# Stage buffers by turns, mirrored key blocks, and another order of loads in a hybrid attention and convolution block

## Chip, core and metric

The kernel runs on one core of a Trainium2 chip. The metric is the device time of one execution in microseconds (us), the median of several executions. All times below are of the kernel before the change.

## What is computed

One residual block over 2048 frames of width 1024, in float32:

```
h = rmsnorm(x, pre_norm_w)
q, k, v, z_att, b, c, u, z_conv, g_att, g_conv = split(h @ w_in)
q, k = partial_rotary(q), partial_rotary(k)            # 8 heads of 64, rotary on 16 of them
pr = softmax(where(chunk(k) <= chunk(q), q k^T / 8, min))   # chunk = 64 frames
a = pr[even heads] - lam * pr[odd heads]               # 4 pairs of heads
att = rmsnorm(a @ v, subln_w) * 0.8 * silu(z_att)
cv = b * causal_conv3(c * u) * silu(z_conv)
m = sigmoid(g_att + bias0) * (att @ w_att_out) + sigmoid(g_conv + bias1) * (cv @ w_conv_out)
out = x + rmsnorm(m @ w_out, post_norm_w)
```

## The kernel before

Every large product is done in three float32r matmuls: each operand is split into a high and a low part (ScalarE copies the high part, VectorE subtracts to get the low one), and TensorE adds high times high, high times low and low times high into one bank of PSUM (`split_product`, lines 889 to 891). All DMAs are issued by one queue, SyncE's (SP), in an order written out by hand; each engine walks its own hand-written program and the programs meet at semaphores. There are four stages.

**First x tiles and V.** The 16 tiles of x (128 rows) are squared and summed (`norm_root`, ScalarE, line 1087, with a Sqrt at line 1090), scaled (`norm`, VectorE, line 1306), transposed (`turn_x`, TensorE, line 899) and split (`ht_split`). The weights of V come in four parts, `wv_raw` 0 to 3, each split into `wv_hi` (line 1106) and `wv_lo`. TensorE's program is `turn_x(0)`, `turn_x(1)`, `turn_x(2)`, V product of tile 0, `turn_x(3)`, V product of tile 1, and so on.

**Line tiles.** 28 tiles of 128 features (z, convolution, queries and keys) times 4 blocks of 512 frames, in the order `SEQ`: tile by tile, but for the last two tiles (p = 26 and 27) block by block, blocks 1, 2, 3, 0, each block with tile 26 and then 27. A block's result is split into one of four buffers, `stage[b]` with b the block, and stored to `qk_s` by 3 DMAs. ScalarE waits for the buffer's last store before it writes it again (`put_out`, line 1161, the ACTIVATE at line 1180). Between these stores SP issues what the next stage needs: keys and queries of the first pair of heads (lines 647 and 632), the weights of gate units 0 to 3 (`load_unit`, line 654; one unit is 24 matmuls, 1 MB of weights), V (line 638).

**Attention and gates.** TensorE does units 0 and 1, then rounds of scores (lines 947, 948), transposes (958), values (975) and a share of the 64 gate units (line 1010). There are 4 pairs of heads with 16 query tiles each. Pairs 1 and 3 go through the query tiles upwards, pairs 2 and 4 downwards. A query tile uses the key blocks (512 frames) up to its own frame, so a pair that goes downwards frees block 3 first and block 0 last, at its end. Key block c lies in `k_sl[c]`, value block c in `v_sl[c]`, and the next pair's block is loaded when the same block of this pair was used for the last time. VectorE masks and takes maxima (1514), ScalarE takes exponentials (1205) and copies finished gate units to `gate_st` (1243), from where SP stores them; before ScalarE copies a unit it waits for the store of the unit two before.

**Merge.** Four blocks of 512 frames. For each, 8 pairs of products (m = 0 to 7, two halves, lines 889 to 891 with `wa` and `br`) go to four banks in turn; the gates are read back through a ring of 5 buffers (`ring_load`, line 806), passed through Sigmoid (line 1269), multiplied (1598) and added (1601), and the sum is split into `m_hi` (1279) and `m_lo` (1603). A ring buffer is loaded again when its last reader is done. In the first block the rows of `w_out` are also loaded (`wo_raw`) and split (`wo_hi` 1282, `wo_lo` 1607), one after each m. Then follow the products with `w_out` (`rows`), Square with a sum (1289), Sqrt, reciprocal, a scaling by it and by `post_w` (1621), the addition of x (1629) and the store.

Of the kernel before, what the change touches and what calls it, by code (L numbers as in the profile page):

```python
# [77 lines left out]
RING = 5  # L78
USES = 2 * KT + 2 * QPB
# [33 lines left out]
def stores_before(p):  # L113
    return NT // 4 + sum(stores_of(x) for x in range(p))

# [15 lines left out]
class Plan:  # L131
# [96 lines left out]
def build(nc, t):  # L228

    with ExitStack() as whole:  # L230
# [86 lines left out]
        k_sl = [held(f"k_sl{i}", [P, 2, BLK], F32R, room) for i in range(NB)]  # L317
# [4 lines left out]
        v_sl = [held(f"v_sl{i}", [P, 2, QPB, VD], F32R, room) for i in range(NB)]  # L322
# [124 lines left out]
        unit_w = [sem(f"unit_w{i}") for i in range(2)]  # L447
        ht_in = [sem(f"ht_in{i}") for i in range(KT // 2)]
# [61 lines left out]
        def _(sp):  # L510
# [83 lines left out]
            def store_block(p, b):  # L594
                kind, j = kind_of(p), place_of(p)
                cs = slice(b * BLK, (b + 1) * BLK)
# [3 lines left out]
                if kind == "z":  # L600
                    sp.dma_start(z_s[p * P:(p + 1) * P, cs], stage[b][:, 0, :]).then_inc(stored[b], 16)
                elif kind == "conv":
                    c0 = (p - CONV_P) // 4 * P
                    sp.dma_start(cv_s[:, c0:c0 + P, cs].rearrange("s p e -> p s e"), stage[b][:]
                                 ).then_inc(stored[b], 16)
                elif j:
                    for lo, hi, row in segments(j):
                        sp.dma_start(qk_s[tile_of(p) // 4, :, row:row + hi - lo, cs].rearrange("s p e -> p s e"),
                                     stage[b][lo:hi]).then_inc(stored[b], 16)
                else:  # L610
                    for half in range(2):
                        rows = qk_s[tile_of(p) // 4, half, :, cs].rearrange("(h r) n -> h r n", r=HD)
                        for a in range(2):
                            sp.dma_start(rows[:, a * HALF:(a + 1) * HALF, :], stage[b][a * HD:(a + 1) * HD, half, :]
                                         ).then_inc(stored[b], 16)
# [14 lines left out]
            def load_k(pair, c):  # L630
                for half in range(2):
                    sp.dma_start(k_sl[c // BLK][half * HD:(half + 1) * HD].bitcast(F32),
                                 qk_s[1, half, pair * P:(pair + 1) * P, c:c + BLK].rearrange("(h j) n -> j h n", h=2)
                                 ).then_inc(k_loaded[c // BLK], 16)

            def load_v(pair, c):
                for half in range(2):
                    sp.dma_start(v_sl[c // BLK][:, half].bitcast(F32),  # L638
                                 v_s[half, c:c + BLK, pair * VD:(pair + 1) * VD].rearrange("(t p) e -> p t e", p=P)
                                 ).then_inc(v_loaded[c // BLK], 16)  # L640
# [10 lines left out]
            def load_unit(u):  # L651
                if u >= 4:
                    sp.wait_ge(unit_done, u - 1)
                sp.dma_start(unit_weights(u)[:].bitcast(F32),
                             split_s[u % GATE_TILES].rearrange("p s (k c) -> p s k c", k=KT)).then_inc(unit_w[u % 2], 16)
# [5 lines left out]
            for i, (p, b) in enumerate(SEQ[-2 * NB:]):  # L661
                store_block(p, b)
                if i == 1:
# [7 lines left out]
                    load_k(0, 0)  # L671
                    load_q(Plan(True), 1)
                if i == 3:
                    sp.wait_ge(proj_done, AT[LINE - 1, 2] + 1)
                    load_unit(0)
                    load_v(0, 0)
                    load_unit(1)
                    for c in range(BLK, S, BLK):
                        load_k(0, c)
                if i == 6:  # L680
                    sp.wait_ge(proj_done, AT[LINE - 2, 0] + 1)
                    load_unit(2)
                    for c in range(BLK, S, BLK):
                        load_v(0, c)
            sp.wait_ge(proj_done, AT[LINE - 1, 0] + 1)
            load_unit(3)
            for s_ in stored:
                sp.wait_ge(s_, 16 * stores_before(LINE))
# [23 lines left out]
            def load_wa(m):  # L712
                sp.dma_start(wa[m][:].bitcast(F32), split_s[GATE_TILES + m].rearrange("p s (k c) -> p s k c", k=KT)
                             ).then_inc(wa_in[wa_group(m)], 16)

# [20 lines left out]
            def attend(plan):  # L736
                gates((0, LEAD))
                for R in plan.rounds:
# [14 lines left out]
                    if R % 2 == 1 and 3 <= R <= TILES + 1:  # L753
# [9 lines left out]
                        for c in gone:  # L763
                            if 2 * B < TILES - NT:
                                load_v(2 * B // NT + 1, c * BLK)
                            elif c:
                                load_branch(0, (None, 7, 0, 1)[c])
# [7 lines left out]
                    for turn, score, value, part in plan.round(R):  # L775
                        gates(part)
                        if score and plan.last_use(G, score[0]):
                            c = score[0] // BLK
                            if pair < VH - 1:
                                sp.wait_ge(qk_done, 2 * (plan.before(G) + c + 1))  # L780
                                load_k(pair + 1, score[0])
                            elif c:
                                sp.wait_ge(qk_done, 2 * (plan.before(G) + c + 1))
                                load_branch(0, 3 + c)

            by_plan(sp, attend)

            def ring_load(n, i):
                b = NB - 1 - n
                place = ring_at(n, i)  # L790
                g = n * USES + i - RING
                if g >= 0:
                    was_n, was = divmod(g, USES)
                    if was >= 2 * KT:
                        sp.wait_ge(y_stored[place], 16 * rows_before(n, i))
# [886 lines left out]
```

## Time and profile before

| | us |
|---|---|
| median of 3 executions | 1841.86 (lowest 1839.49, highest 8872.33) |
| the profiled execution, its own time | 1842.11 |
| its span, first to last instruction | 1840.3 |
| TensorE busy | 1761.2 |
| VectorE busy | 891.5 |
| ScalarE busy | 581.8 |
| GpSimd busy | 89.0 |
| mean granted clock of TensorE | 0.986 of full |

The span is what the trace covers; 1.8 us lie around it. Busy times are sums over the span, so what bounds the kernel is read from the waits of the busiest engine, TensorE, and from what ended them.

### The profile page before, as it was taken

To read this page: it belongs to the slowest core of one execution; us is meant where nothing else is said; L and a number is where in the kernel's file an instruction comes from. 1 tells how busy PE (TensorE), PEld (TensorE's weight loads), DVE (VectorE), ACT (ScalarE), POOL (GpSimd) and SP (SyncE) were. 2 spreads that over 40 slices of the span, in tenths; PEclk is the share of its full clock that TensorE was granted. 3 is DMA by queue.
4 is the path that set the end of the run, shared out by engine and by line. 5 is a ranking of instruction groups with operands and counts; after the bars stand their busy time and mean duration, and the time that the engine had idled before them with its cause. 6 is when DMAs were issued, how large, how long until landed. Compare 5 with 4: busy or idle time off the path is not lost.

```text
span 1840.3 us, 22425 instructions
## 1 busy us (share of the span) xinstructions
PE 1761.2 (96%) x8512; PEld 1469.3 (80%) x8512; DVE 891.5 (48%) x1903; ACT 581.8 (32%) x1040; POOL 89.0 (5%) x74
## 2 busy tenths in 40 slices
PE   6999999999999999699999998999999979999998
PEld 5878888888888888588887887888788758888887
DVE  5538234444334411267666655766666434434252
ACT  5422112121101111144444443444354333313131
POOL 0000000000000000111101112111001000000000
PEclk9999999999999999899999999999999989999999
DMA  6438446465504546776575678657655775353532
GB/s 225 152 129 330 174 160 200 166 206 172 171 12 137 153 122 182 215 218 194 185 201 173 206 227 237 193 177 230 223 169 166 243 239 195 120 180 107 183 104 74
DMA packets 149574, 328.90 MB, mean 179 GB/s; under 512 B 14801, under 2 KB 68049, under 8 KB 135889
## 3 DMA queue, kind: packets, MB, share of 16 engines
q1 hardware_dynamic: 149458, 327.37, 56.3%
q8 instruction: 70, 1.15, 0.3%
q14 instruction: 46, 0.38, 0.1%
HBM read 216.16 MB, written 111.16 MB: 178 GB/s over the span
## 4 chain that ended last, share of the span: by engine, by line
PE 83%; DMA 6%; SPq 4%; ACT 3%; DVE 2%; issue 2%; DVEq 0%; ACTq 0%
PE bank L889 18%; PE bank L890 18%; PE bank L891 18%; PE bank L1010 15%; PE bank L975 5%; PE bank L947 3%; PE bank L948 3%; PE bank L958 2%; ACT e L1205 2%; DMA gate_s<-gate_st 1%; SPq L638 1%; DMA qk_s<-stage 1%; DMA ring<-gate_s 1%; PE bank L899 1%; DVE at_lo L1550 1%
## 5 line engine op out<-in xcount | busy, mean ns | idle before, releaser
L889 PE MATMUL bank<-ht,w 128*128 128x512 f32 x896 | 349.3, 390 | 2.6 <-issue 2.6
L890 PE MATMUL bank<-ht,w 128*128 128x512 f32 x896 | 349.3, 390 | 0.0
L891 PE MATMUL bank<-ht,w 128*128 128x512 f32 x896 | 349.1, 390 | 0.0
L1010 PE MATMUL bank<-ht,w 128*128 128x512 f32 x912 | 239.9, 398 | 1.2 <-DMA w<-split_s 1.2
L889 PEld LDWEIGHTS bank<-ht,w 128*128 128x128 f32 x896 | 168.5, 188 | 38.1 <-ACT w L1118 3.0
L891 PEld LDWEIGHTS bank<-ht,w 128*128 128x128 f32 x896 | 168.6, 188 | 35.1
L890 PEld LDWEIGHTS bank<-ht,w 128*128 128x128 f32 x896 | 168.5, 188 | 35.0
L1010 PEld LDWEIGHTS bank<-ht,w 128*128 128x128 f32 x912 | 168.5, 191 | 33.9 <-DMA w<-split_s 1.4
L1514 DVE CUSTOM_DVE_ANT_0 e<-bank,zeros 128x512 f32<-128x512 f32 x192 | 125.0, 688 | 130.4 <-PE bank L948 129.9
L1205 ACT ACTIVATE e<-e,nbias 128x128 f32<-128x128 f32 (+15 forms) x128 | 152.8, 1196 | 83.7 <-DVE nbias L1523 83.5
L1010 PE MATMUL bank<-hx,w 128*128 128x512 f32 x576 | 156.1, 399 | 3.9 <-DMA w<-split_s 3.9
L947 PE MATMUL bank<-k_sl,q_st 128*128 128x512 f32 (+3 forms) x320 | 129.3, 408 | 21.6 <-DVE stage L1427 8.3
L1214 ACT ACTIVATE at_hi<-bank 128x512 fp32r<-128x512 f32 (+3 forms) x160 | 83.2, 528 | 170.4 <-PE bank L958 170.3
L975 PE MATMUL bank<-at_hi,v_sl 128*128 128x256 f32 (+1 forms) x576 | 117.9, 283 | 12.0 <-DVE at_lo L1550 11.9
L1010 PEld LDWEIGHTS bank<-hx,w 128*128 128x128 f32 x576 | 105.5, 190 | 25.0 <-DMA w<-split_s 5.6
L878 POOL TENSOR_SCALAR mask<-kc,qc 128x128 f32<-128x128 f32 (+3 forms) x64 | 87.5, 1367 | 619.9 <-DVE mx L1514 619.3
L948 PE MATMUL bank<-k_sl,q_st 128*128 128x512 f32 (+3 forms) x320 | 117.1, 370 | 0.0
L889 PE MATMUL bank<-br,wa 128*128 128x512 f32 x256 | 101.0, 395 | 14.3 <-DVE ring L1598 13.6
L975 PEld LDWEIGHTS bank<-at_hi,v_sl 128*128 128x128 f32 x576 | 95.0, 190 | 23.7 <-DVE at_lo L1550 21.5
L1550 DVE TENSOR_TENSOR at_lo<-bank,at_hi 128x512 fp32r<-128x512 f32 (+3 forms) x160 | 97.1, 607 | 31.2 <-ACT at_hi L1214 30.8
L890 PE MATMUL bank<-br,wa 128*128 128x512 f32 x256 | 100.7, 394 | 0.0
L891 PE MATMUL bank<-br,wa 128*128 128x512 f32 x256 | 100.5, 393 | 0.0
(141 smaller groups left out, 2496.7 us busy)
## 6 DMA issues: line engine op xcount, KB each, us to landing
w<-split_s SPq DMA_DIRECT2D x62, 1024.0 KB, 5.4
split_s<-piece SPq DMA_DIRECT2D x24, 1024.0 KB, 5.0
q_st<-qk_s SPq DMA_DIRECT2D x128, 128.0 KB, 5.6
gate_s<-gate_st SPq DMA_DIRECT2D x64, 256.0 KB, 6.0
ring<-gate_s SPq DMA_DIRECT2D x64, 256.0 KB, 3.4
raw<-in_w_in SPq DMA_DIRECT2D x28, 512.0 KB, 6.2
ht_s<-ht SPq DMA_DIRECT2D x3, 4096.0 KB, 27.4
qk_s<-stage SPq DMA_DIRECT2D x48, 192.0 KB
```

Source lines behind the costliest of these rows:

```text
L878: nc.gpsimd.tensor_scalar(mask[m % 2][:, 0:wide], kc[:, c:c + wide], qc[:, plan.tile(G)[1]:plan.tile(G)[1] + 1], MASKED, ALU.is_gt, ALU.mu ...
L889: nc.tensor.matmul(out, left[0], right[0], start=start, stop=False)
L890: nc.tensor.matmul(out, left[0], right[1], start=False, stop=False)
L891: return nc.tensor.matmul(out, left[1], right[0], start=False, stop=stop)
L947: nc.tensor.matmul(out, q_st[G // 2 % 2][:, 0, h, qs], k, start=True, stop=False)
L948: nc.tensor.matmul(out, q_st[G // 2 % 2][:, 1, h, qs], k, start=False, stop=True).then_inc(qk_done, 1)
L975: return nc.tensor.matmul(bank[7][:, q0:QB], v, (at_lo if x == 1 else at_hi)[:, k, q0:QB], start=start, stop=stop)
L1010: mm = nc.tensor.matmul(bank[2 + u % 2][:], unit_weights(u)[:, term // 2, k, :], h_slot(bb, k)[:, term % 2, :], start=i == 0, stop=i == PE ...
L1205: nc.scalar.activation(e, e, ACT.Exp, bias=nbias[G % 2][:, h:h + 1], scale=SCALE, accum_out=esum[G % 2][:, h:h + 1]).then_inc(exp_done, 1)
L1214: nc.scalar.activation(at_hi[:, c // P:(c + wide) // P, q0:q0 + P], bank[5 + o % 2][:, 0:wide].rearrange("p (k n) -> p k n", n=P), ACT.Cop ...
L1514: nc.vector.tensor_tensor_reduce(e[:, c:c + wide], bank[(0, 1, 4)[o % 3]][:, 0:wide], mask[m % 2][:, 0:wide] if masked else zeros[:, 0:wid ...
L1550: nc.vector.tensor_tensor(at_lo[:, ks, q0:q0 + P], bank[5 + o % 2][:, 0:wide].rearrange("p (k n) -> p k n", n=P), at_hi[:, ks, q0:q0 + P]. ...
```

## The change

Four things are changed.

- The results of tiles 26 and 27 go to the stage buffers in the order 2, 3, 0, 1, 2, 3, 0, 1 (`stage_at`), not to the buffer of their block. Waits count the stores into that buffer (`stored_before`). Before attention VectorE waits for buffer 3 alone, not for all four.
- In pairs 3 and 4 of the heads key block c and value block c lie in slot 3 - c (`slot`). During pair 2 the slot that comes free is loaded with block 3 - c of pair 3 (`next_keys`). Buffers of the last stage lie over the slots, so the first merge block's inputs are loaded in the order that fits. The first two gate units get a semaphore of their own.
- At the start the four parts of V's weights are loaded before x tiles 1 to 3, ScalarE loads the table for Sqrt before anything else, and ScalarE and VectorE split V's weights between x tiles 0 and 1. TensorE's program there is unchanged.
- In the first merge block ring buffers 0 and 1 are loaded before the last gate unit is stored, 2 to 4 before any `wa`; `w_out` is loaded later and split later (`WO_AT`: none at m = 0 and 1, then 1, 1, 1, 1, 2 and 2). The row scaling is turned round: VectorE first multiplies by `post_w` in the bank (before the reciprocal is there) and then multiplies by the reciprocal and adds x in one instruction.

```diff
+WO_AT = ((), (), (0,), (1,), (2,), (3,), (4, 5), (6, 7))
...
+def stage_at(p, b):
+    return (2, 3, 0, 1)[(AT[p, b] - AT[LINE - 2, 1]) % 4] if p >= LINE - 2 else b
+
+def stored_before(p, b):
+    return NT // 4 + sum(stores_of(x) for x, y in SEQ[:AT[p, b]] if stage_at(x, y) == stage_at(p, b))
...
+    def slot(self, G, c):
+        return c // BLK if G < TILES // 2 else NB - 1 - c // BLK
+
+    def next_keys(self, G, c):
+        return S - BLK - c if G // NT == 1 else c
...
             for i in range(4):
                 sp.dma_start(wv_raw[i][:], t["w_v"][i]).then_inc(wv_loaded[i], 16)
-                if i < 3:
-                    load_x(i + 1)
+            for i in range(1, 4):
+                load_x(i)
...
                         for c in gone:
                             if 2 * B < TILES - NT:
-                                load_v(2 * B // NT + 1, c * BLK)
+                                load_v(plan, 2 * B // NT + 1, plan.next_keys(2 * B, c * BLK))
...
                             if pair < VH - 1:
                                 sp.wait_ge(qk_done, 2 * (plan.before(G) + c + 1))
-                                load_k(pair + 1, score[0])
+                                load_k(plan, pair + 1, plan.next_keys(G, score[0]))
...
+                sp.wait_ge(qk_done, 2 * plan.before(TILES))
+                for s_ in gate_stored:
+                    sp.wait_ge(s_, 16 * (UNITS - 6) // 2)
+                ring_load(0, 0)
+                ring_load(0, 1)
...
             store_gate(UNITS - 1)
+            sp.wait_ge(pv_done, PAIRS)
+            for i in range(2, RING):
+                ring_load(0, i)
             sp.wait_ge(unit_done, UNITS)
-            sp.wait_ge(pv_done, PAIRS)
+            load_wa(4)
+            for s_ in att_stored:
+                sp.wait_ge(s_, 16 * PAIRS // 2)
+            load_wo(0)
+            load_wo(1)
+            load_wa(5)
             for s_ in gate_stored:
                 sp.wait_ge(s_, 16 * UNITS // 2)
-            for i in range(RING):
-                ring_load(0, i)
-                if i < 4:
-                    load_wa(4 + i)
             for i in range(RING, 2 * KT):
                 ring_load(0, i)
                 if i == RING:
-                    for s_ in att_stored:
-                        sp.wait_ge(s_, 16 * PAIRS // 2)
-                if i < RING + KT:
-                    k = i - RING
-                    sp.dma_start(wo_raw[k][:], t["w_out"][k * P:(k + 1) * P, :]).then_inc(wo_in[k // 2], 16)
+                    load_wa(6)
+                    load_wo(2)
+                    load_wo(3)
+                elif i == RING + 1:
+                    load_wa(7)
+                elif i < RING + 6:
+                    load_wo(i - RING + 2)
...
+            nc.scalar.preload_act_table_set("sqrt_and_others")
             act.wait_ge(consts_ready, 4)
             norm_root(0)
-            norm_root(1)
...
+            split_wv(0)
+            split_wv(1)
             ht_split(0)
+            split_wv(2)
+            split_wv(3)
+            norm_root(1)
+            ht_split(1)
             norm_root(2)
-            ht_split(1)
             norm_root(3)
...
                 if kind != "conv":
-                    act.wait_ge(stored[b], 16 * stores_before(p))
+                    act.wait_ge(stored[st], 16 * stored_before(p, b))
...
-            for s_ in stored:
-                dve.wait_ge(s_, 16 * stores_before(LINE))
+            dve.wait_ge(stored[3], 16 * stored_in_all(3))
...
+                    dve.wait_ge(f_sq, n * 8 + 2 * i + 1)
+                    weigh(0)
                     dve.wait_ge(f_sq, n * 8 + 2 * (i + 1))
                     nc.vector.tensor_tensor(ss[:, 2:3], ss[:, 0:1], ss[:, 1:2], ALU.add).then_inc(f_sum, 1)
+                    weigh(1)
...
-                        nc.vector.tensor_tensor(ring[place][:], bank[4 + o % 4][:], ring[place][:], ALU.add
-                                                ).then_inc(f_out, 1)
+                        nc.vector.scalar_tensor_tensor(out=ring[place][:], in0=bank[4 + o % 4][:], scalar=ss[:, 2:3],
+                                                       in1=ring[place][:], op0=ALU.mult, op1=ALU.add
+                                                       ).then_inc(f_out, 1)
```

## Rows read from the trace of the kernel before

**Rows 1.** The page: busy time, share of the span, instructions of each engine
```profile
PE 1761.2 (96%) x8512; PEld 1469.3 (80%) x8512; DVE 891.5 (48%) x1903; ACT 581.8 (32%) x1040; POOL 89.0 (5%) x74
```
**Rows 2.** Waits of TensorE: total us, times, longest us
```profile
PE bank L899 <- DVE x_n L1306: 16.6, 2, 10.2
PE bank L889 <- DVE ring L1598: 13.6, 1, 13.6
...
PE bank L947 <- DVE stage L1427: 8.3, 1, 8.3
PE bank L947 <- DMA k_sl<-qk_s: 7.2, 1, 7.2
PE bank L947 <- DVE mx L1514: 6.1, 1, 6.1
```
**Rows 3.** Timeline, first 24 us: start us, us, engine, line, instruction [idle before, releaser]
```profile
6.85 1.28 ACT L1090 ACT_TABLE_LOAD   x1
...
9.08 1.06 ACT L1087 ACTIVATE x_n<-x_in 128x1024 f32<-128x1024 f32 x1 [0.64 <-DMA x_in<-in_x]
...
12.99 1.06 ACT L1106 ACTIVATE wv_hi<-wv_raw 128x1024 fp32r<-128x1024 f32 x1 [0.53 <-DMA wv_raw<-in_w_v]
...
17.46 1.06 ACT L1087 ACTIVATE x_n<-x_in 128x1024 f32<-128x1024 f32 x1
...
20.51 1.97 PE L899 MATMUL bank<-ident,x_n 128*128 128x128 f32 x8 [6.41 <-DVE x_n L1306]
...
22.13 0.78 PE L889 MATMUL bank<-wv_hi,ht 128*128 128x512 f32 x1
```
**Rows 4.** Timeline, line tiles to attention, TensorE, ScalarE, SP
```profile
739.70 10.13 PE L1010 MATMUL bank<-ht,first_w 128*128 128x512 f32 x44
...
748.44 1.09 ACT L1180 ACTIVATE stage<-bank 128x512 fp32r<-128x512 f32 x2 [23.38 <-DMA qk_s<-stage]
...
760.42 2.50 PE L1010 MATMUL bank<-ht,w 128*128 128x512 f32 x5 [1.23 <-DMA w<-split_s]
...
763.03 0.77 SPq L654 DMA_DIRECT2D w<-split_s  x1
...
777.14 0.60 ACT L1243 ACTIVATE gate_st<-bank 128x512 f32<-128x512 f32 x1 [2.27 <-PE bank L1010]
```
**Rows 5.** Chain of waits: ten gate matmuls at full clock
```profile
788.91 2.30 PE bank L1010 x10
```
**Rows 6.** Windows: us, busy of each engine, then clock, DMA share, GB/s
```profile
718.00:724.00 6.00, 6.00 (x28) 4.99 (x27) 0.00 (x0) 0.03 (x1) 0.00 (x0) 1.00 0.76 206
...
726.00:746.00 20.00, 20.00 (x90) 16.57 (x89) 0.00 (x0) 0.00 (x0) 2.53 (x4) 1.00 0.95 260
...
750.00:770.00 20.00, 4.58 (x13) 3.61 (x14) 2.19 (x10) 3.06 (x5) 0.29 (x1) 0.67 0.93 269
```
**Rows 7.** Landing times of the weights of units 2 and 3
```profile
DMA to landing us min/median/max: 7.1/7.8/8.4
```
**Rows 8.** Chain of waits between pairs 2 and 3
```profile
1113.17 4.13 PE bank L1010 x14
```
**Rows 9.** Chain of waits, first merge block
```profile
1474.98 10.61 DMA ring<-gate_s
...
1513.93 4.05 DMA ring<-gate_s
...
1520.01 3.95 DMA ring<-gate_s
```
**Rows 10.** Timeline, first merge block: TensorE, ScalarE, VectorE
```profile
1467.98 0.50 PE L889 MATMUL bank<-br,wa 128*128 128x512 f32 x1 [0.69 <-ACT gate_st L1243]
...
1495.10 1.06 ACT L1282 ACTIVATE wo_hi<-wo_raw 128x1024 fp32r<-128x1024 f32 x1 [8.25 <-DMA wo_raw<-in_w_out]
...
1536.29 1.23 DVE L1607 TENSOR_TENSOR wo_lo<-wo_raw,wo_hi 128x1024 fp32r<-128x1024 f32 x1 [0.26 <-ACT wo_hi L1282]
```
**Rows 11.** Timeline, end of the output, VectorE
```profile
1836.47 1.28 DVE L1629 TENSOR_TENSOR ring<-bank,ring 128x512 f32<-128x512 f32 x2
```

More of the change, by code:

```diff
@@ L316, in build @@
         q_st = [held(f"q_st{b}", [P, 2, 2, QB], F32R, room) for b in range(2)]
[L317 removed]
+        k_sl = {i: held(f"k_sl{i}", [P, 2, BLK], F32R, room) for i in (3, 0, 1, 2)}
         sub = ExitStack()
@@ L447, in build @@
         unit_w = [sem(f"unit_w{i}") for i in range(2)]
+        first_in = [sem(f"first_in{i}") for i in range(2)]
         ht_in = [sem(f"ht_in{i}") for i in range(KT // 2)]
@@ L714, in load_wa, with ring_load @@
                              ).then_inc(wa_in[wa_group(m)], 16)
+            def ring_load(n, i):
+                b = NB - 1 - n
+                place = ring_at(n, i)
+                g = n * USES + i - RING
+                if g >= 0:
+                    was_n, was = divmod(g, USES)
+                    if was >= 2 * KT:
+                        sp.wait_ge(y_stored[place], 16 * rows_before(n, i))
+                    elif was % 2:
+                        sp.wait_ge(m_sum, was_n * KT + was // 2 + 1)
+                    else:
+                        sp.wait_ge(m_lo_done, was_n * KT + was // 2 + 1)
+                if i < 2 * KT:
+                    r0 = (i % 2) * D + (i // 2) * P
+                    src = gate_s[r0:r0 + P, b * BLK:(b + 1) * BLK]
+                else:
+                    r0 = b * BLK + (i - 2 * KT) // 2 * P
+                    src = t["x"][r0:r0 + P, (i % 2) * 512:(i % 2) * 512 + 512]
+                sp.dma_start(ring[place][:], src).then_inc(ring_loaded[place], 16)
             def gates(part):
@@ L1319, in _, with split_wv @@
             dve.wait_ge(consts_ready, 4)
-            norm(0)
-            norm(1)
-            for r in range(4):
+            def split_wv(r):
                 dve.wait_ge(w_hi_done, r + 1)
@@ L1604, in _ @@
                                             ).then_inc(m_lo_done, 1)
-                    if n == 0:
-                        dve.wait_ge(wo_hi_done, m + 1)
-                        nc.vector.tensor_tensor(wo_lo[m][:], wo_raw[m][:], wo_hi[m][:].bitcast(F32), ALU.subtract
+                    for k in WO_AT[m] if n == 0 else ():
+                        dve.wait_ge(wo_hi_done, k + 1)
+                        nc.vector.tensor_tensor(wo_lo[k][:], wo_raw[k][:], wo_hi[k][:].bitcast(F32), ALU.subtract
                                                 ).then_inc(wo_lo_done, 1)
@@ L1619, in _ @@
                         o = 2 * i + half
-                        bk = bank[4 + o % 4][:]
-                        nc.vector.scalar_tensor_tensor(out=bk, in0=bk, scalar=ss[:, 2:3],
-                                                       in1=post_w[:, half * 512:half * 512 + 512], op0=ALU.mult,
-                                                       op1=ALU.mult).then_inc(f_scaled, 1)
-                    for half in range(2):
-                        o = 2 * i + half
                         place, count = ring_at(n, 2 * KT + o), ring_count(n, 2 * KT + o)
```

124 lines of the change are left out of this document (63 added, 61 removed).

## The prediction

> **What bounds the kernel now.** I read the page first: TensorE is busy 1761.2 of 1840.3 us [rows 1]. So the question is where it is not busy, and the view of its waits answers that [rows 2]: six waits make 51.8 us of the 79 that are left. Two stand at the very start (16.6), one is in the first merge block (13.6), two are between line tiles and attention (8.3 and 6.1), one is between pairs 2 and 3 of the heads (7.2). The timeline and the chain of waits around each show who was late. The change touches each of these places and nearly nothing else, so I go through them in order of time. I count against the profiled execution's own 1842.1 us, which is 0.2 above the median of the runs.
>
> A wait costs more than its length: after a long idle stretch TensorE's matmuls run at half clock. Ten gate matmuls take 2.30 us at full clock [rows 5], five after a stop take 2.50 [rows 4]. I therefore price a stall from the last matmul before it to a point behind it where the clock is full again, and compare with the same work at 0.23 us a matmul.
>
> **The start.** V's first product stands at 22.13, right behind the transposes of x tile 2 at 20.51 [rows 3], since TensorE's program has them first. They follow the Square of tile 2 (17.46) by 3.05 us. Today that Square waits behind the four weight splits. What lands when: x tile 1 is the fourth load and there at 9.08; the part of `wv_raw` that is seventh is there at 12.99. After the change x tile 1 is seventh, so I take 13.0 for it. Then: its Square at 13.0, its transposes 3.05 later at 16.05, its ScalarE split behind these (2.5 us until the second half is done, taken as for tile 2), Square of tile 2 at 18.55, its transposes at 21.6, V's product at 23.2. That is **+1.1 us**. Two table loads of 1.28 us [rows 3] leave the chain of tile 0, but tile 0 is early then and waits for tile 1: this part is worth nothing. Bounds: -1.5 (x tile 1 lands earlier than the rank says) and +1.5.
>
> On the landing order the Trainium skill, DMA: Bandwidth & Descriptors, section "Queues, rings and completion order", says that completion is not first in, first out for one issuing engine. By that rule tile 1 may overtake weights, and the term would be nearer to its lower bound; the nine landings in this trace came in issue order.
>
> **Line tiles to attention.** Stage buffer b serves tile 26 and then tile 27 of the same block, so ScalarE stood 23.38 us until a store landed [rows 4], and TensorE, whose units 0 and 1 ended at 739.70 + 10.13 = 749.83, waited 8.3 us for the last block. Then VectorE waited for all stores: 6.1 us more [rows 2], with 1.23 for unit 2's weights between [rows 4]. With four buffers by turns, each buffer's store is two blocks of 10.9 us old when it is needed. Both waits go. The whole stretch from 749.83 to the end of unit 2 at 777.14 [rows 4] holds 24 gate matmuls (5.5 us) and 13 small ones (1.8), 7.3 us at full clock: a possible gain of 27.3 - 7.3 = 20.0.
>
> What is late next is the DMA queue. Its engines are busy 0.95 in 726 to 746 and 0.93 in 750 to 770 [rows 6]; before and between, SP had nothing to issue because the stores waited. The first batch (units 0 and 1, V's first block, keys, two stores) is 19.0 us of work, the second (stores, units 2 and 3, the rest of V) starts at about 750.5. In the changed kernel the first follows straight on what fills 0.76 of 718 to 724 [rows 6], at about 722.8, and the second straight on the first at 741.8. Unit 3's weights were issued at 763.03 and took 8.4 us [rows 4, 7], so they landed 20.9 us after their batch began; less 0.8 us, since that batch was not full at its beginning, that gives 761.9. Unit 2's landed at 760.4 and now land, by the same shift, at 751.6 (wait 1.3 behind the first scores). TensorE wants unit 3 at 749.83 + 1.3 + 7.3 = 758.4 and gets it at 761.9: it waits 3.5 us. Against the 777.14 of before that is 15.2. ScalarE's copy of unit 2 needs the store of `gate_st` 0, which SP can issue only when all stage stores have landed (about 759.5); it lands at about 763.5, and exponentials and `at_hi` are queued behind that wait, but TensorE's next value product comes at 766.4, which is just late enough. For a new dip of the clock I take off 1.1: **-14.1 us**. Bounds: -20.0 (the queue keeps up) and -9 (the gate store 3 us later and two dips of 2 us, eleven matmuls at 0.43 instead of 0.23, less what overlaps).
>
> **Pairs 2 and 3.** Key block 0 of pair 3 can be loaded only when pair 2 has used its own block 0 for the last time, and is needed one query tile later: 7.2 us [rows 2], then fourteen gate matmuls in 4.13 us [rows 8] instead of 3.22 and about 1.5 us lost on the small ones before them. Mirrored, block 0 goes into the slot that pair 2 frees first, twelve query tiles ahead. The loads are as many and at the same places in SP's order; block 3 takes the late slot and is needed twelve tiles on. 7.2 + 0.9 + 1.5 = **-9.6 us**; bounds -7 (no clock gain, something small in its place) and -10. Next late are the weights for the gates, which were issued before the keys.
>
> **First merge block.** Its first product starts at 1467.98, one takes 2.72 us, and four banks let it run to the sixth (1484.3). Then it waits 13.6 for the third product's gating [rows 2], because VectorE and ScalarE stand in their programs behind `wo_raw` 0 and 1, which land at 1495.10 [rows 10]. Before that, ring buffer 3 landed only at 1474.98 + 10.61 = 1485.6, behind three `wa` [rows 9]. From m = 2 on a turn sets the pace: a ring load of 4.05, then Sigmoid, `m_hi` and `m_lo`, and 6.08 us after the last load the next [rows 9]. Eight turns and the splits of `w_out` end with `wo_lo` 7 at 1537.5 [rows 10].
>
> After: rings 0 to 4 have landed by 1475, so `m_lo` 0 hangs on the second product and (1473.4, then 2.8 for gating, adding and both splits) ends at 1476.2 instead of 1487.6. Ring 5 is issued then, behind two `wa` and two `wo_raw` (3.1 MB; the loaded 10.61 us above were for three `wa` and three rings, 3.9 MB, so I take 0.36 MB a us): it lands at 1483.6, `m_lo` 1 is done at 1485.5. Ring 7 goes then, behind two `wa`, two `wo_raw` and ring 6: it lands at 1493.7, `m_lo` 2 ends at 1495.7. TensorE loses 2.6 us at its eleventh product. Five turns of 5.8 (6.08 with the queue's gaps) bring `m_lo` 7 to 1524.7, and with the last two splits `wo_lo` 7 to 1527.3: **-10.2 us**, a wait of 13.6 turned into several small ones. Carried through at 0.30 MB a us the end is 5.3 us earlier than now, at 0.40 12.7: these are the bounds.
>
> **The tail.** After the last reciprocal come two multiplications and then two additions, these 1.28 us until 1837.75 [rows 11]. After: the pair of additions is gone, since two combined instructions take the multiplications' place, and one multiplication by `post_w` (0.64) comes ahead of the reciprocal, half of it beside the Sqrt. 1.28 - 0.35 = **-0.9 us**; in the other blocks this work lies beside TensorE's and costs nothing (0 to -1).
>
> **Sum.** 1.1 - 14.1 - 9.6 - 10.2 - 0.9 = -33.7; 1842.1 - 33.7 = **1808.4 us**, 1.8% less.
>
> **Rivals.** *The queue keeps up.* Stage rotation is then worth the full 20.0 and the merge 12.7: 8.4 more, 1800.0; part of it gives 1800 to 1805. For it: the loads in the merge ran faster, 3.9 MB in 10.61 us, than the 260 to 269 GB/s of these batches [rows 6, 9]; against it: both batches hold the same stores and loads as before, and their engines were full.
> *The backlog bites harder.* The gate store lands late, ScalarE's queue holds the exponentials, and both short waits halve the clock: rotation 9, merge 5.3: 1818.4. The Trainium skill, TensorE: Matmul & The Clock Gate, section "HAM oscillation — how this bites in real kernels", describes a kernel in which each short wait for a DMA puts the array back to half clock. By that rule this rival is the likelier one; of this trace only the long waits are followed by slow matmuls [rows 4, 8].
> *A wait only moves.* Behind the keys another load is late and pair 3 gains nothing: 1818.
> *Slower than before.* The ring's turn in the merge: every ring load is now issued among 8.4 MB of weights. If each of the seven later turns had a loaded ring of 10.6 us [rows 9] and 2.0 behind it, `m_lo` 7 would end at 1476.2 + 7 x 12.6 = 1564.4, `wo_lo` 7 at 1567, 29.5 later than now; with the other terms (-23.5) that is 1848. It turns into a loss at a load of about 9.8 us a turn. Against it: the weights are enough for two or three such turns only.
>
> **How the numbers follow.** Forecast 0.50, with a range of its own of 1805 to 1813; queue keeps up 0.26; backlog 0.17; a wait only moves 0.04; slower than before 0.03. The range 1801 to 1817 leaves out about 2 in 10. Two per cent (36.8 us, to 1805.3) is about what a measurement of this kernel can tell from no change. Below it lie the first rival and a little of the forecast, less the part of the rival just above: 0.28. Slower by over 2%: 0.01. The rest 0.71.
>
> **What would show it.** In the changed trace: V's first product at 23.2; ScalarE's copy of (27, 3) and (27, 0) without a wait for a store; TensorE past 749.8 + 1.1 with a wait for unit 2's and one of 3 to 4 us for unit 3's weights, and DMA share near 1 without a gap between 727 and 763; no wait at line 947 for keys; in the merge no long wait but several of 1 to 3 us, ring loads 5 and 7 of about 7 us, and a turn near 6. The prediction is wrong if unit 3's weights are there at 759 (5 us less), or if ScalarE stands for the gate store past 766 (up to 5 us more), or if the merge's turns stay above 7 us.

## The result, and the profile after

The changed kernel takes 1816.3 us, median of its four runs, against 1843.5 for the kernel before, measured with it: a ratio of 0.986, 95% interval 0.985 to 0.988, so 1.4% faster. One run of each (2945 and 8872 us) was disturbed and is left out of the ratio; without it the medians are 1815.6 and 1841.9. The profiled execution took 1817.1 us of its own time, span 1815.3. The forecast was 1808.4, so 7 to 9 us of the promised 33.7 are missing.

TensorE's waits after the change (the view of waits: total us, times, longest us), under the page's line of busy times:

```profile
PE 1759.0 (97%) x8512; PEld 1467.5 (81%) x8512; DVE 893.9 (49%) x1903; ACT 581.3 (32%) x1039; POOL 89.2 (5%) x74
```
```profile
PE bank L945 <- DVE x_n L1362: 17.8, 3, 8.0
PE bank L1021 <- DVE at_lo L1609: 11.7, 16, 2.2
PE bank L1059 <- DMA w<-split_s: 9.9, 5, 3.8
PE bank L935 <- DVE ring L1657: 6.8, 2, 4.7
...
PE bank L993 <- DMA q_st<-qk_s: 0.9, 1, 0.9
```

Line 993 is 947 of before, 935 is 889, 1059 is 1010. The three waits at line 947 (8.3, 7.2, 6.1) are gone, and the 13.6 of the merge is now 6.8 [rows 2]. But the waits for gate weights have grown from 5.1 to 9.9, and a wait for a query tile is new. To place the difference I compare the two traces at events that both have: V's first product, and ScalarE's copy of each of the 64 gate units, which marks how far TensorE has come. Each start is read from the timeline.

| event | before | after | after - before | this stretch |
|---|---|---|---|---|
| V's first product | 22.13 | 23.32 | +1.2 | +1.2 |
| copy of gate unit 3 | 785.80 | 773.88 | -11.9 | -13.1 |
| unit 30 | 1097.16 | 1084.28 | -12.9 | -1.0 |
| unit 31 | 1116.43 | 1093.81 | -22.6 | -9.7 |
| unit 32 | 1124.99 | 1103.93 | -21.1 | +1.6 |
| unit 60 | 1445.06 | 1424.40 | -20.7 | +0.4 |
| unit 63, the last | 1467.34 | 1450.30 | -17.0 | +3.6 |
| last copy into `m_hi` | 1791.82 | 1767.77 | -24.1 | -7.0 |
| span | 1840.3 | 1815.3 | -25.0 | -0.9 |

**Start** (timeline, as [rows 3]):
```profile
12.79 1.06 ACT L1136 ACTIVATE x_n<-x_in 128x1024 f32<-128x1024 f32 x1
...
16.16 1.97 PE L945 MATMUL bank<-ident,x_n 128*128 128x128 f32 x8 [6.26 <-DVE x_n L1362]
...
21.70 1.97 PE L945 MATMUL bank<-ident,x_n 128*128 128x128 f32 x8 [3.57 <-DVE x_n L1362]
...
23.32 0.78 PE L935 MATMUL bank<-wv_hi,ht 128*128 128x512 f32 x1
```
The Square of x tile 1 comes at 12.79, as ScalarE ends its splits and as the tile lands (issued at 3.68, 9.1 us to landing by the view of the DMAs), and no longer at 9.08, and the turns at 16.16 and 21.70 follow as worked out.

**Line tiles to attention** (timelines of TensorE, ScalarE, SP; then the windows, as [rows 6]):
```profile
751.71 1.43 PE L1059 MATMUL bank<-ht,w 128*128 128x512 f32 x5 [0.42 <-DMA w<-split_s]
...
762.57 3.35 PE L1059 MATMUL bank<-ht,w 128*128 128x512 f32 x7 [3.77 <-DMA w<-split_s]
```
```profile
763.26 0.60 ACT L1299 ACTIVATE gate_st<-bank 128x512 f32<-128x512 f32 x1 [6.45 <-DMA gate_s<-gate_st]
```
```profile
739.01 13.39 SPq L667 DMA_DIRECT2D v_sl<-v_s  x6
752.44 1.74 SPq L635 DMA_DIRECT2D qk_s<-stage  x3
754.23 0.47 SPq L683 DMA_DIRECT2D w<-split_s  x1
```
```profile
726.00:746.00 20.00, 20.00 (x90) 16.55 (x89) 2.39 (x5) 3.79 (x6) 2.54 (x4) 1.00 1.05 295
...
750.00:770.00 20.00, 15.81 (x66) 12.61 (x66) 8.23 (x35) 4.91 (x16) 5.35 (x4) 0.83 0.93 276
```
TensorE works through to 751.3, waits 0.42 for unit 2's weights and 3.77 for unit 3's, and then does seven gate matmuls in 3.35 us where full clock takes 1.6. ScalarE stands 6.45 us for the store of the gate buffer. SP's view has what stands ahead of unit 3's weights: SP needs 13.39 us to issue six value loads (1.57 MB), in a stretch in which the DMA engines are busy all the time (share 0.99 from 739.0 to 752.4, 318 GB/s), and the stage stores and unit 3's weights come behind them.

**Pairs 2 and 3, and gate unit 61** (timeline, TensorE; then the chain of waits):
```profile
1099.95 0.45 PE L993 MATMUL bank<-k_sl,q_st 128*128 128x384 f32 x1 [0.95 <-DMA q_st<-qk_s]
...
1435.71 4.56 PE L1059 MATMUL bank<-hx,w 128*128 128x512 f32 x12 [2.56 <-DMA w<-split_s]
```
```profile
1424.40 11.27 DMA w<-split_s
```
No key is waited for. Before, unit 61's weights took 9.26 us and TensorE waited 0.56; now they take 11.27, it waits 2.56, and twelve gate matmuls take 4.56 instead of 3.02 us (granted clock 0.63 from 1435.7 to 1440.3, where before it was 1.00 over the same twelve).

**First merge block** (timeline of SP, chain of waits, timeline of TensorE):
```profile
1448.70 0.86 SPq L764 DMA_DIRECT2D ring<-gate_s  x2
1455.30 0.33 SPq L723 DMA_DIRECT2D gate_s<-gate_st  x1
```
```profile
1449.66 5.63 issue
...
1456.14 4.69 DMA ring<-gate_s
...
1462.91 9.48 DMA ring<-gate_s
...
1474.41 6.92 DMA ring<-gate_s
```
```profile
1475.13 0.47 PE L935 MATMUL bank<-br,wa 128*128 128x512 f32 x1 [2.13 <-DVE ring L1657]
...
1485.55 0.77 PE L935 MATMUL bank<-br,wa 128*128 128x512 f32 x1 [4.71 <-DVE ring L1657]
```
The chain is a chain of ring loads. Ring 3 lands at 1460.8, ring 5 needs 9.5 us, ring 7 6.9. SP issues the last gate store 5.0 us after ScalarE's copy began (1450.30). The tail's last instruction pair starts at 1811.35 and is one pair instead of two.

### The profile page after: what moved, and what is told of

Its sections match the earlier page's. It is cut to its first block, busy times and chain, and to the rows that moved or that the text cites. A ratio compares the mean times of both kernels' runs of the same rounds, so it can differ in the third digit from the quotient of the medians.

```text
span 1815.3 us, 22423 instructions
## 1 busy us (share of the span) xinstructions
PE 1759.0 (97%) x8512; PEld 1467.5 (81%) x8512; DVE 893.9 (49%) x1903; ACT 581.3 (32%) x1039; POOL 89.2 (5%) x74
## 4 chain that ended last, share of the span: by engine, by line
PE 86%; DMA 4%; ACT 3%; SPq 3%; DVE 2%; issue 2%; DVEq 0%; ACTq 0%
PE bank L935 19%; PE bank L936 19%; PE bank L937 19%; PE bank L1059 15%; PE bank L1021 5%; PE bank L993 3%; PE bank L994 3%; PE bank L1004 2%; SPq L667 2%; ACT e L1261 2%; DMA ring<-gate_s 1%; DMA w<-split_s 1%; PE bank L945 1%; DMA gate_s<-gate_st 1%; DVE at_lo L1609 1%
## 5 line engine op out<-in xcount | busy, mean ns | idle before, releaser
L1021 PE MATMUL bank<-at_hi,v_sl 128*128 128x256 f32 (+1 forms) x576 | 118.1, 284 | 11.9 <-DVE at_lo L1609 11.7
```

What stands on the lines that cost most here:

```text
L1021: return nc.tensor.matmul(bank[7][:, q0:QB], v, (at_lo if x == 1 else at_hi)[:, k, q0:QB], start=start, stop=stop)
```

## Experiments

A stretch without an edit can differ between two profiles by about 1 us (from the last gate copy to the last `m_hi` it was up to 1.2 apart), and in two profiles it was 2 to 2.5 us, so I read medians and ratios together with the ledger. All ratios are to the kernel before, measured in the same batch of runs as the version.

| version | median us | ratio, 95% |
|---|---|---|
| changed | 1816.3 | 0.986 (0.985 to 0.988) |
| start undone | 1815.0 | 0.986 (0.984 to 0.987) |
| stage undone | 1827.5 | 0.993 (0.991 to 0.994) |
| keys undone | 1821.7 | 0.989 (0.986 to 0.991) |
| merge undone | 1821.4 | 0.989 (0.987 to 0.990) |
| values late | 1810.8 | 0.984 (0.982 to 0.986) |
| rings late | 1812.8 | 0.985 (0.983 to 0.987) |
| norms first | 1808.3 | 0.983 (0.981 to 0.984) |
| tiles swapped | 1811.9 | 0.983 (0.981 to 0.985) |
| `w_out` behind | 1813.1 | 0.984 (0.983 to 0.986) |
| four edits | 1798.5 | 0.976 (0.974 to 0.978) |
| four edits, rings late | 1796.4 | 0.976 (0.973 to 0.978) |
| the same again | 1798.6 | 0.976 (0.975 to 0.978) |

### Each part undone

**Start.** x loads between the weight parts again, no early table load, norm of tile 1 ahead of the splits.
```
+                if i < 3:
+                    load_x(i + 1)
-            for i in range(1, 4):
-                load_x(i)
...
-            nc.scalar.preload_act_table_set("sqrt_and_others")
```


> The changed kernel with only the loads and the order of the first x tiles put back as they were before. Theory A (the parts' costs stand apart and add up; the start was worth +1.1 in the forecast and +1.2 by the traces): V's first product comes back from 23.3 us to about 22.1, and the run takes 1815.1 against 1816.3 for the changed kernel. Rival: the early table load was worth its 1.28 us and the late loads of x cost more than 1.2, with the lot hidden behind V's products: then the first product moves and the gate copies of the first units do not, and the run stays at 1816.3.

V's first product came at 21.98, and every gate copy 1.1 to 2.7 us sooner than in the changed kernel. So the traces have the start as a loss of some 1.3 us that is not hidden behind V's products: theory A. The medians alone do not show it: they fell by 1.3, or by 0.6 from 1815.6, and the intervals of the two ratios overlap nearly whole.

**Stage.**
```
-    return (2, 3, 0, 1)[(AT[p, b] - AT[LINE - 2, 1]) % 4] if p >= LINE - 2 else b
+    return b
...
-            dve.wait_ge(stored[3], 16 * stored_in_all(3))
+            for i, s_ in enumerate(stored):
+                dve.wait_ge(s_, 16 * stored_in_all(i))
```


> The changed kernel with only the stage buffers of the last line tiles used as before (buffer of its own block every time, and VectorE waiting for every store). Theory A (the waits for stage buffers are the whole of this part): the wait of 8.3 us and its like come back between 725 and 765 us, the third gate unit starts 13 later, and the run takes about 1829.4 (1816.3 + 13.1; 1830.4 with the forecast's 14.1). Rival (the backlog of loads sets the end of this stretch whatever the stage does, so that mirrored keys and the rest already hide part of it): under 7 us, 1823 or less.

Both waits are back (view of waits):
```profile
PE bank L993 <- DVE stage L1487: 8.3, 1, 8.3
...
PE bank L993 <- DVE mx L1574: 6.0, 1, 6.0
```
Unit 3's copy comes 13.6 us later, 13.4 of it in this stretch. The median rose by 11.2, less by 1.7 that unit 61 gave back (no slow matmuls there). The waits for stage buffers are the whole of this part.

**Keys.**
```
-        return c // BLK if G < TILES // 2 else NB - 1 - c // BLK
+        return c // BLK
...
-        return S - BLK - c if G // NT == 1 else c
+        return c
...
-                                load_branch(0, (None, 1, 0, 7)[c])
+                                load_branch(0, (None, 7, 0, 1)[c])
```


> The changed kernel with only the keys of pairs 3 and 4 loaded and used in the old order (and the slots and branch loads that go with it). Theory A (each of the two turns from one head pair to the next costs a reload of the block that was used last): the wait of 7 to 10 us at the turns near 1040 to 1110 us comes back for both, the short wait for a query stage of 0.95 us at 1100 goes, and the run takes 1824.5 (1816.3 + 8.2), 1825.9 if the new wait of 0.95 has another cause and stays. If the 3.6 us lost at gate units 61 and 62 hang on the mirrored keys, these come back too: 1821.

```profile
PE bank L993 <- DMA k_sl<-qk_s: 6.2, 1, 6.2
```
The wait is back, at one turn and not at two (my expectation was loose: pairs 3 to 4 never waited), and unit 31 is 9.6 us later, 9.0 of it between units 30 and 31. At unit 32 this shrinks by 1.5: the wait for queries at 1099.95 is gone with the mirroring. So the new wait is a consequence of it. At units 61 to 63 it shrinks by another 3.8, with this row:
```profile
1441.63 3.02 PE L1059 MATMUL bank<-hx,w 128*128 128x512 f32 x12 [0.41 <-DMA w<-split_s]
```
The loss at unit 61 hangs on this part. The median rose by 5.4, near the 1821 that I gave for that case.

**Merge.** The loads one after another as before.
```
-                ring_load(0, 0)
-                ring_load(0, 1)
...
+            for i in range(RING):
+                ring_load(0, i)
+                if i < 4:
+                    load_wa(4 + i)
...
-WO_AT = ((), (), (0,), (1,), (2,), (3,), (4, 5), (6, 7))
+WO_AT = tuple((m,) for m in range(8))
```


> The changed kernel with only the loads of the merge in their old order (none before the last pair's values, output weights one after each ring load). Theory A (early rings and late output weights are worth 7.1 us by the traces, 10.2 in the forecast): 1823.4, the ring wait of 10.6 us back, and the last gate store issued about 1 us after ScalarE's last gate copy instead of 4.4 us after. Theory B (the early ring loads also take the 3.6 us at gate units 61 and 62): these come back here, so that the undo costs only 3.5 us: 1819.8, and the weights for the unit at 1435 land in 9.3 us and not 11.3.

From the last gate copy to the last `m_hi` 7.5 us more than changed, with a ring wait of 14.2 us; the median rose 5.0, or 4.4 by the ratios, where 7.1 was expected. This profile was 2.5 us ahead at the first gate copy, before anything edited; whether the other runs were too is not known. The wait at unit 61 stayed (2.30, then 4.38 for twelve matmuls): theory B is out.

### The late weights of unit 61

Across all traces the wait follows one thing: which operand tile of the merge is read just before the 1 MB tile `wa` 3. In eight traces (changed, start, stage and merge undone, values late, rings late, norms first, `w_out` behind) three attention tiles stand there and TensorE waits 2.3 to 3.1 us; before and keys undone have a conv tile and two attention tiles, and wait 0.6 and 0.4. So I swapped two tiles, in memory and in the order of loads.
```
-        for k in (7, 0, 1):
+        for k in (1, 0, 7):
             late_br(k)
...
-                                load_branch(0, (None, 1, 0, 7)[c])
+                                load_branch(0, (None, 7, 0, 1)[c])
```


> The changed kernel with two of the merge's operand tiles in each other's place in memory and in the order of loads: the load just ahead of the last weight tile of 1 MB near 1419 us is a conv tile again (7), as before the change, and the attention tile (1) comes later. Five profiles with three attention tiles there show TensorE waiting 2.3 to 2.7 us for the weights of gate unit 61, two with one conv and two attention tiles 0.4 and 0.6. Theory A (which tile is read there makes the difference): the wait falls to about 0.5 us, the half clock after it goes in the runs that had it, and the run takes 2 to 3.6 us less than 1816.3, some 1813.5. Rival (it is the mirrored keys, by the addresses or times of their loads): the wait stays at 2.3 us or more and the run at 1816.

```profile
1432.84 3.02 PE L1059 MATMUL bank<-hx,w 128*128 128x512 f32 x12 [0.16 <-DMA w<-split_s]
```
The wait is 0.16; unit 63 gains 4.0 us on unit 60, and the median falls by 4.4. `wa` 3 lands in 10.4 us instead of 12.8 (12.5 to 13.3 in the eight, 10.8 before, 10.6 with keys undone) with the same bytes in the same places of SP's order. The swap changes both what is read and where in memory it is written; which of these matters was not separated.

### The stage stretch: value loads ahead of weights

```
                     load_unit(2)
-                    for c in range(BLK, S, BLK):
-                        load_v(Plan(True), 0, c)
...
+                    for c in range(BLK, S, BLK):
+                        if R == (2 * c // BLK - 1 if plan.causal else -1):
+                            load_v(plan, 0, c)
```


> The changed kernel with the value blocks 2 to 4 of the first pair of heads loaded one at a time in the rounds of the loop that use them first, and not all before the weights of gate unit 3. Theory A (TensorE's wait of 3.77 us at 762.57 is the queue of issues on SP ahead of unit 3's weights, and those 6 value loads took SP 13.4 us to issue): the weights are issued some 10 us sooner, the wait goes and the slow clock after it too: 4 to 6 us less, 1811.3. Rival (the bytes that are under way set the landing, not the order of the issues): the wait stays at 2 to 4 us or moves to the scores or values that follow, and the run takes 1815 to 1817.

SP, and what is left of TensorE's waits up to 765:
```profile
743.04 0.45 SPq L683 DMA_DIRECT2D w<-split_s  x1
```
```profile
752.87 1.43 PE L1060 MATMUL bank<-ht,w 128*128 128x512 f32 x5 [1.30 <-DMA w<-split_s]
```
Unit 3's weights are issued 11.2 us sooner and nobody waits for them. How long they take to land, from the view of the DMAs at their issue, changed kernel and then this run:
```profile
w<-split_s SPq DMA_DIRECT2D x1, 1024.0 KB, 8.3
```
```profile
w<-split_s SPq DMA_DIRECT2D x1, 1024.0 KB, 13.5
```
So they land at 756.5 instead of 762.5: 6.0 us sooner, and not 11.2. Unit 3's copy comes 5.1 us sooner; the next unit's weights are now waited for 1.05 us, and the copies from unit 4 on come 3.4 to 5.8 sooner. The median fell by 5.5. The outcome is theory A's, its mechanism only in part: SP is free sooner, but the six value loads are also 1.57 MB that no longer stand ahead of the weights, and at the 318 GB/s of the changed kernel from 739.0 to 752.4 they are 4.9 us, by my estimate, most of the 6.0. This run does not part the time at which a load is issued from the bytes ahead of it.

### The start: norms ahead of the splits

```
             norm_root(0)
             split_wv(0)
-            split_wv(1)
+            norm_root(1)
             ht_split(0)
+            split_wv(1)
+            norm_root(2)
+            ht_split(1)
             split_wv(2)
             split_wv(3)
-            norm_root(1)
-            ht_split(1)
-            norm_root(2)
             norm_root(3)
```
with VectorE's program in the same order and the x loads between the weight parts.

> The changed kernel with the x tiles loaded in turn with the parts of V's weights, as before the change, the early table load kept, and ScalarE and VectorE taking the norm of x tile 1 before the second part of the weights and the norm of tile 2 before the turn of tile 1 is copied. Theory A (the first V product waits for the turned tiles 0 and 1, not for the last part of the weights): V's first product comes 3 to 5 us sooner than 23.3 us, 1811.3 to 1813.3. Rival (V's first block then waits for x tiles 2 and 3 instead, so that only the start moves): first product 3 us or more sooner, the end under 1.5 us sooner, 1814.8 to 1816.3.

```profile
17.52 0.78 PE L935 MATMUL bank<-wv_hi,ht 128*128 128x512 f32 x1
```
V's first product is 5.8 us sooner, and so is every gate copy up to unit 1 (5.8). The median fell by 8.0 (6.4 by the ratios), in excess of that: the rest is spread over later waits, 2.2 of it at units 2 and 3, and I can't say that the start caused it. Whether the early table load, worth nothing as changed, pays here was not tested: it was only kept.

### The merge: late exit and loads ahead of ring 5

With `ring_load(0, 0)` and `(0, 1)` behind the last gate store:

> The changed kernel with ring loads 0 and 1 of the merge issued after the last gate store and not before it. Theory A (the early loads of 256 KB each are under way when SyncE and ScalarE leave the block of gate units, and the instructions they need next come over the same DMA engines, which costs them 2.4 to 3.5 us): the last gate store is issued about 1 us after ScalarE's gate copy instead of 4.4, the table load comes 2.4 us sooner, and the merge ends within 1 us of the changed kernel or up to 2 us sooner: 1814.3 to 1817.3. Rival (the delay has nothing to do with these loads, it comes from SyncE's longer program behind the block): store and table load stay 4.4 and 4.6 us behind, and the later rings only add up: 1817.5 to 1820.

```profile
1452.18 0.33 SPq L723
...
1454.01 7.42 DMA ring<-gate_s
...
1463.50 6.80 DMA ring<-gate_s
```
In the chain of waits the last gate store goes out 1.6 us after the gate copy began (1450.61) instead of 5.0. To the end of that issue it is 1.75 to 1.9 us in the five traces without early rings (before, merge undone, rings late, the four edits with late rings and their repeat) and 5.0 to 5.6 in the nine with them. So the early rings hold up SyncE as it leaves the block of gate units, and ScalarE too: its table load starts 2.7 to 3.5 us after the copy in the five and 4.3 to 5.3 in the nine. What they gain, 0.3 us at `m_lo` 0 (it starts 12.1 against 11.8 us after the copy), is lost: `m_lo` 1 starts at 21.0 instead of 23.4. The time is the same or a little less: 1812.8 is below the 1814.3 to 1817.3 of theory A, but the intervals of the two ratios overlap.

The mechanism is only argued: in the 4.9 us after the copy the DMA view lists four packets of the queues of kind "instruction" (16 KB each or less) between the ring's packets; before, with the short exit, it lists five, so it is not their number. The Trainium skill, Runtime: NRT & Kernel Launch, section "Instruction fetch mechanics", says that each sequencer fetches its instructions in blocks over a DMA queue of its own and that a taken branch out of the loaded blocks stops it until the block is there. By that rule both engines stop at this exit in every version. That the stop is longer with ring loads under way is what the rows show, and no run shows the fetch to be its cause.

Then the weights in front of ring 5:
```
             load_wa(4)
-            load_wo(0)
-            load_wo(1)
             load_wa(5)
...
                 if i == RING:
-                    load_wa(6)
-                    load_wo(2)
-                    load_wo(3)
+                    load_wo(0)
+                    load_wo(1)
                 elif i == RING + 1:
-                    load_wa(7)
+                    load_wa(6)
+                elif i == RING + 2:
+                    load_wo(2)
+                    load_wo(3)
+                    load_wa(7)
```


> The changed kernel with the first output weights (512 KB each, 2 of them) issued behind ring load 5 and not ahead of it, the next ones behind ring load 7. Theory A (ring 5 needed 9.5 us to land because 3 MB were queued ahead of it): it lands in 6 to 7.5 us, m_lo 1 is ready 20 to 21 us after the last gate copy instead of 23.4, m_lo 2 at 27 to 30 instead of 32.3, and the run takes 1.5 to 4 us less, 1813.5. Rival (the traffic of the whole stretch is the bound, so the order only moves which load is late): m_lo 1 is sooner, a wait for w_out or for a weight tile takes its place, and the run stays at 1816.

Its chain of waits:
```profile
1461.51 4.72 DMA ring<-gate_s
...
1468.26 5.49 DMA ring<-gate_s
```
Rings 5 and 7 land in 4.7 and 5.5 us instead of 9.5 and 6.9; `m_lo` 1 and 2 start 19.8 and 27.3 us after the gate copy instead of 23.4 and 32.3. Of these 5 us only 2.0 reach the last `m_hi`: the turns after them take 7.7, 6.0 and 5.8 us instead of 6.3, 5.2 and 5.1, and TensorE waits 4.3 for rings and 2.2 for `wo_lo`. The median fell by 3.3. So the theory holds for ring 5, and the rival for more than half of the gain.

### The four together

> The changed kernel with four edits at once: the start in turns with the norms ahead (8.0 us less alone), value blocks loaded in the round that uses them (5.5 less alone), the operand tiles swapped and the output weights behind ring 5. Theory A (the parts lie in four stretches and add up): 1816.3 - 8.0 - 5.5 - 2.8 - 2.8 = 1797. Rival (part of each was a late load that a sooner start runs into: the loads have no more time when everything ahead of them is quicker): 1800 to 1804.

> The same four edits, and rings 0 and 1 issued after the last gate store. Theory A (the early ring loads give 1 us at the first merge turn and cost as much by holding up SyncE and ScalarE as they leave the gate block): within 1.5 us of the version with early rings. Rival (with output weights out of the way the early rings are worth their 5 us of headstart): 2 to 3 us slower than the version with early rings.

> The version with the four edits and the late rings once more, on whatever chip it falls, for a closer figure. If it is the fastest of all, its ratio to the kernel before is 0.9755 to within 0.002 and its time 1794 to 1799 us; if its first figure was luck, it comes out with the version with early rings or above, at 1799 or more.

1798.5, 1796.4 and 1798.6 us: 2.4% faster than before and about 18 us faster than the changed kernel, of 21 that the single medians add up to. The first is near the 1797 of theory A and below the rival's 1800, so the parts nearly add up. In the early version TensorE waits 4.4 us for gate weights at 1287.57 (2.4 in the changed kernel), but in the two late ones 1.8 and 1.7 at about the same total, so where the other 3 us went is open. Early and late rings can't be told apart (0.9757 and 0.9755), nor can the repeat (0.976), so the early ones are not worth their lines.

## Why the prediction was right or wrong

The forecast of 1808.4 was 8 us too low; 1816.3 lies outside the forecast's own range of 1805 to 1813, at the upper edge of the whole one, and not by the rival that led there: "the backlog bites harder" wanted 9 us from the stage rotation, and this gave 13.1. Between the traces 8.8 us of the sum did not come. 3.6 of them are the weights of gate unit 61, which the sum does not have; 3.2 the first merge block, where "rings 0 to 4 have landed by 1475" failed; 1.5 a query load that became late behind the keys; 1.0 the wait for unit 3's weights with the slow matmuls behind it. By the terms, predicted and measured between the traces:

| term | predicted | measured |
|---|---|---|
| start | +1.1 | +1.2 |
| stage rotation | -14.1 | -13.1 |
| keys | -9.6 | -8.1 |
| unit 61 | 0 | +3.6 |
| first merge block | -10.2 | -7.0 |
| tail | -0.9 | -0.9 |
| else | 0 | -0.6 |

**Start: right,** to 0.1 us, and confirmed by its undoing. Tile 1 was taken to land at 13.0 and landed at 12.8, and the nine first loads landed in issue order again. The rule on completion order of the Trainium skill, DMA: Bandwidth & Descriptors, section "Queues, rings and completion order", by which tile 1 might have overtaken weights, did not come into play; with ScalarE's splits ending at the same time it would have gained nothing either.

**Stage rotation: right in mechanism, 1.0 too large.** The wait for unit 3's weights was forecast at 3.5 and was 3.77; they were used at 762.57, forecast 761.9. The clock after it cost more than the 1.1 set aside: seven gate matmuls alone lost 1.7. The gate store landed where it was said (763.5 against 763.26). What I did not see is that this wait was avoidable: another order of the same loads removed it.

**Keys: the wait went, and one came.** "The loads are as many and at the same places in SP's order" was true, and is the reason for the loss: the query tile at 1099.95 was loaded at the same place too, but TensorE arrived 9.7 us earlier and used up the slack that the key wait had given it. This 0.95 and the work around it, 1.6 us in all, is the difference. I asked only what the gate weights would do.

**Unit 61: missed altogether, 3.6 us.** The failed step is the sentence that the change touches "nearly nothing else": the order of the merge's operand loads, which followed from the mirroring, is in no term of the sum, so it was costed at nothing. The swap shows that it was worth 4 us; why one order is slower stays open.

**First merge block: 3.2 too much.** Right were the pattern (no long wait but two of 2.1 and 4.7) and, to 0.3 us, the pace of the last five turns (5.5 against 5.8). Wrong was the time of `m_lo` 0. "Rings 0 to 4 have landed by 1475" is 7.0 us after the merge's first product, and `m_lo` 0 was to end at 8.2; both took the last gate store and rings 2 and 3 to go out at once. They went out 3.5 us later than before relative to the copy, as in every trace with early rings; ring 3 landed at 9.9, and `m_lo` 0 was done 11.9 us after the first product: 3.7 late. Ring 5, forecast at 7.4, needed 9.5: 2.1 more. Ring 7 gave back 1.3 (6.9 for 8.2) and the five turns 1.4, which leaves 3.1 of the 3.2.

**The rivals.** The turn of the ring at 10 us or more never came. "A wait only moves" happened in small: of 9.7 us 1.6 moved to the queries. The rule on repeated half clock of the Trainium skill, TensorE: Matmul & The Clock Gate, section "HAM oscillation — how this bites in real kernels", was named for "backlog": in the eight traces with a wait of 2.3 to 3.1 us ahead of unit 61, the twelve gate matmuls after it took 4.4 to 5.5 us in four and 3.0 to 3.1 in the other four. So here it holds for half of the waits of this size, which are shorter than the 3 to 5 us of the kernel that the section describes. Two per cent is also not what a measurement of this kernel can just tell from no change, as the prediction had it: the ratio's interval is 0.3% wide and lies wholly below 1.

## What to carry to other kernels

When a stall is removed, list every load that is issued at a fixed place and is first used after the stall: each has lost that much slack, not only the one next in line. Order loads in a full queue by the time at which they are needed, one at a time: loads that are wanted much later hold up SP's program and put their bytes ahead of the others; this was worth 5.5 us without a byte less in all. Look at what is issued just before engines leave a branch: here 0.5 MB of loads went with an exit some 3 us longer.

## What the runs showed of the hardware

- SP can be held up by its own DMAs: six value loads of 256 KB took 13.39 us to issue while the DMA engines' share was 0.99, where with the values moved the three stage stores and unit 3's weights went out between 741.68 and 743.49. Issued 11.2 us sooner, the weights landed 6.0 us sooner (13.5 us from issue to landing instead of 8.3).
- As SyncE leaves the block of gate units, the issue of the last gate store ends 1.75 to 1.9 us after the start of the copy that it stores and, with 0.5 MB of ring loads just issued, 5.0 to 5.6 (five traces and nine).
- The same wait for a DMA is followed by half clock in one run and by full clock in another (twelve gate matmuls in 4.56 or 3.04 us after waits of 2.56 and 2.62; granted clock 0.63 and 1.00).
- Two tiles of 512 KB in each other's place, in the order of loads and in memory, changed the landing of the 1 MB tile behind one of them from 12.8 to 10.4 us; which of the two places matters was not separated.
